# Expert rows scattered to two tables from where they lie, four token tiles summed on TensorE, and constant products placed in ten of TensorE's waits

## The reference, cut to what matters

```python
x = x + mod[:, 2] * (concat([ya, yb, yn]) @ w_out)
h2 = rms_norm_2(x, g2) * (1 + mod[:, 4]) + mod[:, 3]
grp = argmax(h2 @ w_rg + b_rg)                    # one of 4 groups
top_v, top_i = top_k(logit_e[grp], 2)             # 2 of its 8 experts
gate = softmax(top_v) * p_grp
y_e = (silu(g) * u) @ w_down[e],  g, u = split(h2 @ w_up[e])   # 32 experts, hidden 512
f = gate_0 * y_{e0} + gate_1 * y_{e1}             # two experts of each token
out = rms_norm_2(x + mod[:, 5] * f, final_g)
```

## Time and profile before

| What | Value |
|---|---|
| Median of the runs | 2865.32 us (2862.7 to 2867.55) |
| The profiled execution, its own time | 2869.49 us |
| Its span in the profile | 2867.5 us |
| Mean granted TensorE clock | 0.979 |
| TensorE busy | 2743.7 us, 96% |
| VectorE, ACT, POOL busy | 53%, 27%, 3% |
| Moved by DMA | 399.56 MB, 139 GB/s over the span |

### The profile page before, as it was taken

The page is one execution under the profiler, slowest core; times in us unless marked ns, Lnnn a source line. Parts: engine busy times, 40 slices in busy tenths (PEclk is TensorE's granted clock), DMA queues, the critical chain, the costliest instruction groups (busy, mean ns, idle before and its releaser), DMA issues. The chain is left out here.

```text
span 2867.5 us, 44001 instructions
## 1 busy us (share of the span) xinstructions
PE 2743.7 (96%) x18171; PEld 1635.5 (57%) x18171; DVE 1510.6 (53%) x2119; ACT 781.6 (27%) x1449; POOL 83.7 (3%) x138
## 2 busy tenths in 40 slices
PE   8999899999999999999999998999999799999995
PEld 4444554444444444444454445657555699999994
DVE  7886676566666667773652007867683311111114
ACT  2111771111111114511100106757332311211112
POOL 0000000000000000000000000000000011111110
PEclk9999999999999999999999998999999899999997
DMA  3022221111111117764221000004200799999996
GB/s 142 33 74 38 47 90 69 50 44 44 45 44 44 45 50 267 275 240 144 59 61 64 30 0 12 1 1 120 97 12 10 302 395 399 386 403 396 392 397 255
DMA packets 75940, 399.56 MB, mean 139 GB/s; under 512 B 13232, under 2 KB 22960, under 8 KB 59824
## 3 DMA queue, kind: packets, MB, share of 16 engines
q1 hardware_dynamic: 55440, 348.66, 33.1%
q10 hardware_dynamic: 13104, 32.52, 3.2%
q0 software_dynamic: 7280, 16.79, 1.7%
HBM read 362.66 MB, written 29.36 MB: 137 GB/s over the span
## 5 line engine op out<-in xcount | busy, mean ns | idle before, releaser
L3646 PE MATMUL ex_ps<-big,ex_xT 128*32 128x128 f32 x3072 | 348.9, 274 | 0.0
L3644 PE MATMUL ex_ps<-big,ex_xT 128*32 128x384 f32 x3072 | 344.7, 489 | 1.4 <-issue 0.7
L3646 PEld LDWEIGHTS ex_ps<-big,ex_xT 128*32 128x32 f32 x3072 | 333.7, 110 | 0.6
L1756 PE MATMUL ffn_ps<-h,V 128*128 128x512 f32 x504 | 219.7, 592 | 0.0
L2215 PE MATMUL ffn_ps<-big,V 128*128 128x512 f32 x484 | 211.3, 597 | 3.6 <-DVE V L2470 1.4
L296 DVE TENSOR_SCALAR_CACHE_REDUCE h<-ad_s_ps 128x1280 f32<-128x1280 f32 x64 | 92.9, 1489 | 177.2 <-PE ad_s_ps L205 177.2
L3644 PE MATMUL ex_ps<-ex_wd,ex_hT 128*32 128x384 f32 x1536 | 173.4, 492 | 4.3 <-DMA ex_wd<-in_w_edown 1.9
L3646 PE MATMUL ex_ps<-ex_wd,ex_hT 128*32 128x128 f32 x1536 | 175.5, 275 | 0.0
L3646 PEld LDWEIGHTS ex_ps<-ex_wd,ex_hT 128*32 128x32 f32 x1536 | 168.4, 111 | 0.6
L1756 PEld LDWEIGHTS ffn_ps<-h,V 128*128 128x128 f32 x504 | 95.8, 190 | 120.5 <-issue 120.5
L2215 PEld LDWEIGHTS ffn_ps<-big,V 128*128 128x128 f32 x484 | 92.2, 191 | 120.3 <-issue 115.0
(11 more groups left out here) (606 smaller groups left out, 4792.6 us busy)
## 6 DMA issues: line engine op xcount, KB each, us to landing
big<-in_w_eup SPq DMA_DIRECT2D x64, 2048.0 KB, 26.4
ex_wd<-in_w_edown SPq DMA_DIRECT2D x32, 2048.0 KB, 27.4
V<-in_w_down SPq DMA_DIRECT2D x35, 704.0 KB, 5.6
dn_tail<-in_w_mod ACTq DMA_DIRECT2D x48, 512.0 KB, 5.0
fm_up<-in_w_up SPq DMA_DIRECT2D x22, 1028.0 KB, 4.9
dn_tail<-in_w_in SPq DMA_DIRECT2D x17, 512.0 KB, 4.4
big<-y_dram SPq DMA_DIRECT2D x16, 512.0 KB, 7.0
f_w<-in_w_in SPq DMA_DIRECT2D x14, 512.0 KB, 4.3
```

The costliest lines, as they stand in the source:

```text
L1756: mm = nc.tensor.matmul(bank(i, j), wj[:, k, :], bj[:, k, :], start=(k == 0), stop=(k == 3))
L3644: nc.tensor.matmul(o[32 * g:32 * g + 32, 0:W], rows(g), w[:, 0:W], start=first, stop=last)
L3646: mm = nc.tensor.matmul(o[BR:P, g * P:(g + 1) * P], rows(g), w[:, W:BANK], start=first and g == 0, stop=last and g == GR - 1)
```

## The change

Four edits.

1. The table `y_dram` becomes two, `y_wide` with 768 columns and `y_rest` with 256. ACT's moves go. POOL waits for `y_kept` itself and issues four indirect DMAs for a block: one for the 768 columns of 96 rows, three for the 256 columns of 32 rows each, straight from partitions 96 to 127. Their row numbers have to stand at partitions 0 to 31, so route makes them in a second layout (`thirds`: two small turns on TensorE and one VectorE instruction), and POOL copies them beside the others.
2. At the end each tile of 128 tokens is read by two DMAs, and all tiles in the order 0, 4, 1, 5, 2, 6, 3, 7. For tiles 0 to 3 TensorE also sums the second weighted row (`weighted(t, 1, ...)`, with a diagonal of the second gates, `diag1`), and ACT and VectorE take these tiles out of PSUM. VectorE's `mix` remains for tiles 4 to 7.
3. `busy` makes products of two constants of 512 columns whose result nobody reads; it is called at ten places of TensorE's code.
4. `out_rows` moves into a spare part of a large buffer.

```diff
+def busy(nc, cst, bank, count):
+    for _ in range(count):
+        nc.tensor.matmul(bank, cst["ident"], cst["ones_on"], start=True, stop=True)
 attention:
                 scores(0)
+                if packed:
+                    busy(nc, cst, o_banks[0], 3)
                 scores(1)
+                if packed:
+                    busy(nc, cst, o_banks[0], 3)
 ...
                 values(I // 4 - 1)
+                busy(nc, cst, s_ps[:, 0, 0, 0:BANK], 2)
 dilated_attention, at the end:
+                busy(nc, cst, s_ps[:, 0, 0, :], 1)
 near_attention:
                 scores(0)
+                busy(nc, cst, o_ps[:], 1)
                 scores(1)
 front, at the end:
+                wait_kept(pe, J["v", 6])
+                busy(nc, cst, acc[:, J["v", 6] % 2, 0:BANK], 4)
 mid, token_sums:
                     begin(("tok",))
+                    busy(nc, cst, slot(("tok",))[:, 0:BANK], 2)
                     pe.wait_ge(sum_added, KD)
 gla_and_out, at the end:
+                busy(nc, cst, ps[:, 3, :], 2)
 route:
                 nc.tensor.matmul(tot_ps, cst["ones"], total, start=True, stop=True).then_inc(pre_ready, 1)
+                pe.wait_ge(evicted, TT)
+                busy(nc, cst, acc[:, 1, 0:BANK], 7)
 ...
                 nc.tensor.transpose(ids_ps[0:BR], listed[:], cst["ident"][0:NB, 0:NB]).then_inc(ids_ready, 1)
+                for g in range(1, GR):
+                    mm = nc.tensor.transpose(third_ps[0:32, g - 1, 0:NB], listed[:, 32 * g:32 * g + 32], cst["ident"][0:NB, 0:NB])
+                mm.then_inc(ids_ready, 1)
+                busy(nc, cst, acc[:, 1, 0:BANK], 8)
 experts, SP:
-                    for t in (4, 0, 5, 1, 6, 2, 7, 3) if a == 0 else range(TT):
-                        sp.dma_start(f[:, t, :], y_dram[a * T + t * P:a * T + (t + 1) * P, :]).then_inc(got[t], 16)
+                    for t in order:
+                        tile = slice(a * T + t * P, a * T + (t + 1) * P)
+                        sp.dma_start(f[:, t, 0:2 * W], y_wide[tile, :]).then_inc(got[t], 16)
+                        sp.dma_start(f[:, t, 2 * W:D], y_rest[tile, :]).then_inc(got[t], 16)
 experts, POOL, scatter:
+                    nc.gpsimd.tensor_copy(third_at[0:32, u], r["thirds"][0:32, :, bass.ds(i * 2 + u, 1)]).then_inc(row_set, 1)
-                    pool.wait_ge(moved[u], i * (16 * GR) + 16 * GR)
+                    pool.wait_ge(y_kept, i * 2 + (u + 2))
-                    pool.indirect_dma_start(y_dram, bass.IndirectOffsetOnAxis(ap=row_at[0:BR, u:u + 1], axis=0), y[0:BR, u, :], None,
+                    pool.indirect_dma_start(y_wide, bass.IndirectOffsetOnAxis(ap=row_at[0:BR, u:u + 1], axis=0), y[0:BR, u, :], None,
                                             bounds_check=2 * T - 1, oob_is_err=False).then_inc(stored[u], 16)
+                    for g in range(GR):
+                        at = third_at[0:32, u, g - 1, :] if g else row_at[0:32, u:u + 1]
+                        pool.indirect_dma_start(y_rest, bass.IndirectOffsetOnAxis(ap=at, axis=0), y[BR:P, u, g * 2 * P:(g + 1) * 2 * P], None,
+                                                bounds_check=2 * T - 1, oob_is_err=False).then_inc(stored[u], 16)
 experts, TensorE:
+                def weighted(t, a, f, got):
+                    pe.wait_ge(got[t], 32)
                     for half in range(2):
+                        mm = nc.tensor.matmul(sum_ps[t][:, half, :], r["diag1"][t] if a else r["diag"][:, t, :],
+                                              f[:, t, half * BANK:(half + 1) * BANK], start=False, stop=(a == 1))
 experts, ACT:
-                def move_y(i, u):
-                    act.wait_ge(y_kept, i * 2 + (u + 2))
-                    for g in range(GR):
-                        act.dma_start(y[32 * g:32 * g + 32, u, 2 * W:D], y[BR:P, u, g * 2 * P:(g + 1) * 2 * P]).then_inc(moved[u], 16)
 experts, VectorE:
+                for n, t in enumerate(order):
                     if t < PET:
+                        mix(t + PET)
+                    finish(n, t)
```

More of the change, by code:

```diff
@@ L3489, in _, with experts @@
                 V_.tensor_scalar(r["rows"][0:BR, :], ids_ps[0:BR], 2.0 * T, None, ALU.add)
-def experts(nc, tag, cst, din, r, ids, h2_dram, y_dram, wu, u_ready, xb, x_ready, f0, f1, y, hid, a2, shift, h, rows, out):
+                dve.wait_ge(ids_ready, 2)
+                V_.tensor_scalar(r["thirds"][0:32], third_ps[0:32, :, 0:NB], 2.0 * T, None, ALU.add)
+def experts(nc, tag, cst, din, r, ids, h2_dram, tables, wu, u_ready, xb, x_ready, f0, f1, y, hid, a2, shift, h, rows, out):
     H = 512
@@ L3504, in experts @@
         xT = ph.sb("xT", [P, 2, KD, BR])
-        idx, row_at = ph.sb("idx", [P, 2], I32), ph.sb("row_at", [P, 2], I32)
+        idx, row_at, third_at = ph.sb("idx", [P, 2], I32), ph.sb("row_at", [P, 2], I32), ph.sb("third_at", [P, 2, 2, 1], I32)
         W = 4 * BR
+        SCATTERS = 1 + GR
+        y_wide, y_rest = tables
+        order = [t for pair in zip(range(PET), range(PET, TT)) for t in pair]
         hT = ph.sb("hT", [P, GR, P])
@@ L3514, in experts @@
         d_ready = [ph.sem("d_ready0"), ph.sem("d_ready1")]
-        moved, stored = [ph.sem("moved0"), ph.sem("moved1")], [ph.sem("stored0"), ph.sem("stored1")]
+        stored = [ph.sem("stored0"), ph.sem("stored1")]
         got0, got1 = ([ph.sem(f"got{a}_{t}") for t in range(TT)] for a in range(2))
@@ L3568, in _ @@
                     sp.wait_ge(y_free, pairs * 2 + (a + 1))
[L3569 to L3572 removed]
+                    for t in order:
[3 more added lines that the diff above has]
+                for n, t in enumerate(order):
+                    sp.wait_ge(finished, n + 1)
                     sp.dma_start(out[t * P:(t + 1) * P, :], f1[:, t, :]).then_inc(out_stored, 16)
@@ L3734, in _ @@
                 pe.wait_ge(xT_ready, pairs * 2 + 2)
-                token_sum(0)
-                token_sum(1)
-                token_sum(2)
-                pe.wait_ge(y_kept, pairs * 2 + 1)
-                token_sum(3)
+                for t in range(PET):
+                    if t == PET - 1:
+                        pe.wait_ge(y_kept, pairs * 2 + 1)
+                    residual(t)
+                    weighted(t, 0, f0, got0)
+                for t in range(PET):
+                    weighted(t, 1, f1, got1)
             @block.scalar
@@ L3825, in weigh @@
                     V_.tensor_tensor(r["diag"], cst["ident"].unsqueeze(1).broadcast_to([P, PET, P]),
-                                     gate[:, 0, 0:PET].unsqueeze(2).broadcast_to([P, PET, P]), ALU.mult).then_inc(gates_ready, 1)
+                                     gate[:, 0, 0:PET].unsqueeze(2).broadcast_to([P, PET, P]), ALU.mult)
+                    for t in range(PET):
+                        ins = V_.tensor_scalar(r["diag1"][t], cst["ident"], gate[:, 1, t:t + 1], None, ALU.mult)
+                    ins.then_inc(gates_ready, 1)
                 def keep_hidden(i, u):
@@ L3925, in experts_block @@
         h2_dram = nc.dram_tensor("h2_dram", (T, D), F32).ap()
-        y_dram = nc.dram_tensor("y_dram", (2 * T, D), F32).ap()
-        blk, ids, out_rows = keep("blk", [P, NB], I32), keep("ids", [P, NBI], I32), keep("out_rows", [P, NB], I32)
+        y_wide, y_rest = (nc.dram_tensor(x, (2 * T, n), F32).ap() for x, n in (("y_wide", 8 * BR), ("y_rest", D - 8 * BR)))
+        blk, ids = keep("blk", [P, NB], I32), keep("ids", [P, NBI], I32)
         count, first_expert = keep("count", [P, 3], I32), keep("first_expert", [P, 1], I32)
-        small = big[:, 20, 4 * P:4 * P + 9 * TT]
+        small = big[:, 20, 4 * P:8 * P]
         r = {"g4": small[:, 0:4 * TT].rearrange("p (t g) -> p t g", t=TT), "top": small[:, 4 * TT:5 * TT],
-             "gate": small[:, 5 * TT:7 * TT].rearrange("p (a t) -> p a t", a=2), "std": small[:, 7 * TT:8 * TT], "swapped": small[:, 8 * TT:9 * TT], "rows": out_rows[:], "block": blk[:], "count": count[:], "ids": ids[:], "first": first_expert[:],
+             "gate": small[:, 5 * TT:7 * TT].rearrange("p (a t) -> p a t", a=2), "std": small[:, 7 * TT:8 * TT], "swapped": small[:, 8 * TT:9 * TT],
+             "rows": small[:, 9 * TT:9 * TT + NB], "thirds": small[:, 9 * TT + NB:9 * TT + 3 * NB].rearrange("p (g n) -> p g n", g=2),
+             "diag1": [big[:, (18, 21)[t // 2], 8 * BR + t % 2 * P:8 * BR + (t % 2 + 1) * P] for t in range(4)], "block": blk[:], "count": count[:], "ids": ids[:], "first": first_expert[:],
              "gate5": big[:, 18, 0:8 * BR], "final": big[:, 19, :], "diag": big[:, 20, 0:4 * P].rearrange("p (t n) -> p t n", n=P)}
```

68 lines of the change are left out of this document (30 added, 38 removed).

## The result

The changed kernel takes 2928.72 us (median of 4 runs, 2924.65 to 2931.15), the kernel before beside it 2866.44 us (2862.70 to 2871.59): a ratio of 1.0215, 95% interval 1.0194 to 1.0236. I had forecast 2849.5 us. The profiled execution spans 2922.8 us instead of 2867.5, 55.3 us more.

The account below looks back on a forecast made before the run. TensorE bounds the kernel up to 2280 us, TensorE and DMA engines the experts, then a closing chain. 5.9 + 4.7 + 5.3 = 15.9 us won, from a median of 2865.32 to 2849.5 us; range 2841 to 2861.

Parts of the forecast that it names:

- part 1: Expert stage: dropping the moves inside SBUF for four scatters a block relieves the DMA engines and wins 5.9 us.
- 8.2 of 17 us ... Hidden: Expert stage: POOL's four issues, index copies and gather take 8.2 us of a 17 us block, so they stay hidden.
- The third rival: Expert stage: POOL becomes the bound from 3.65 us an issue; at 4.0 us the time is 2897 us; chance 0.05.
- 0.05 for slower: Whole kernel: chance given to a measurement slower than before, against 0.85 for faster and 0.10 for same.
- the range of 2841 to 2861: Whole kernel: forecast range in us, said to leave out the slow case and the far ends.
- DMA relief, 5.9 us: Expert stage: the DMA need falls from 17.5 to 17.3 us a block, so TensorE's whole 5.9 us excess goes.
- the moves' 1.8%: Expert stage: the removed moves' share of DMA time, taken as 9.7 us over 540 us; upper bound 9 us won.
- The end, 4.7 us: After the last y kept: 2.8 us from earlier scatters plus 1.9 us from the tiles; bounds 0 and 7.
- the bare sum: Closing tiles: VectorE takes four pairs at 4.3 us, 17.2 against 21.5, before about 1 us taken back by DMAs.
- my sum: End: the four scatters overlap, the last landing at 2836.0 instead of 2838.84 us, not four times 3.19 us in series.
- Constant products, 5.3 us: TensorE's waits: ad 4.4, near attention, route and mid 1.0 each, less 2.1 at phase ends; bounds -4 and 12.
- Parts 1 and 2: Expert stage scatters, 5.9 us won, and the end after the last y kept, 4.7 us won.

Follow-up runs that it names:

- kernel 8: Changed kernel with each of a block's four scatters let go at its own event, 2 to 6 us apart; 2852.06 us, ratio 0.9942 to the kernel before.
- kernel 12: kernel 8 without any of the constant products; 2854.92 us, ratio 0.9964 to the kernel before.
- kernel 2: The kernel before with the constant products alone added; 2860.04 us, ratio 0.9980 to the kernel before.
- (5): Changed kernel with two scatter issues in a row per block instead of four, same packets and bytes; 2865.45 us (one run).
- (3): Changed kernel with a block's four scatters in two pairs, the second waiting for the next up product; 2877.75 us, ratio 1.0039 to the kernel before.

## Why the prediction was wrong, by its own steps

**The step that failed** is in part 1: "8.2 of 17 us ... Hidden". I priced POOL's four issues as POOL's own time only and put their cost to TensorE at nothing. As POOL's own time the sum was even high: the four take 4.5 us (2331.19 to 2335.65), not 5.8, and POOL is busy 5 us of 19.4. Still the row of four makes the block 2.4 us longer than TensorE's 17.0. From the experts' first turn to the last y kept it is 626.1 us, 63.2 more than before, and 71.6 more than kernel 8 with the same issues apart (554.5, from 2255.48 to 2810.03). The cost stood on an engine whose waits name nothing of POOL's. The third rival, the slow case, had the right instructions and the wrong mechanism: its condition was an issue over 3.65 us, and issues took 0.87 to 0.93 us. So 0.05 for slower was far too low, and its 2897 us rested on a supposed 4.0 us an issue.

What could have warned: nowhere in the rows of before do more than two indirect issues follow each other. The one pair at 1.45 us lies in route, where TensorE waits for another reason, and in the experts two issues are 2.0 us apart. I took from these that issues overlap with everything else. No trace row showed four in a row beside a TensorE fed with short products. So "Hidden" had nothing measured behind it, and the range of 2841 to 2861 left the cost out. How POOL's issues reach TensorE stays open; the runs show that their spacing decides.

**DMA relief, 5.9 us: right.** With the issues apart the period is 17.01 us to the end. In kernel 12 the experts' first turn to the last y kept takes 556.6 us (2255.79 to 2812.36) instead of 562.9, 6.4 us won. One slip of the working: the moves' 1.8% is a share of the 608 us of the earlier trace rows, 10.9 us and not 9.7; it changes the upper bound and not the 5.9.

**The end, 4.7 us: 3.3 in one profile of each kernel, from terms that were each off.** From y kept to the second table's reads it is 11.5 us (2884.57 to SP's read at 2896.10) against 13.0, as the last scatter lands 5.41 us behind its issue, not 3.19: 1.4 us won where I said 2.8. From that read to the first mix it is 5.9 us against 3.3, 2.6 us lost where I said 1.3: the wait ends with the second piece of the second tile, whose read is issued 1.3 us behind the first (2897.41 against 2896.10) and takes 4.47 us where the one before took 3.17. VectorE's part, 2901.97 to 2918.95, is 17.0 us against 21.5, the bare sum: 4.5 us won where I said 3.2, for stores and double DMAs took nothing back. 1.4 - 2.6 + 4.5 = 3.3.

The Trainium skill ("DMA: Bandwidth & Descriptors", Rules for kernel authors) says that many small transfers should be coalesced and that one under 64 KB is mostly overhead. In series, at the 3.19 us of before, that would have been 12.8 us, from 2886.4 to 2899.2; the last landed at 2896.0, so they overlap in part, and the trace stands between the rule and my sum. The loss in the stage is another matter: with 64 bytes a row or 1 KB it is the same 19.39 us a block.

**Constant products, 5.3 us: about 6 us by the ratios (0.2% in kernel 2, and 0.2% between kernels 8 and 12), the mechanism in part unproven.** The scores in ad are as forecast, but kernel 12 has most of that gain without a product. Its experts start at 2255.79 us, earlier than the changed kernel's 2258.46, so the 4.6 us by which these came forward are no measure of the products. One thing was put at nothing and shows: with the 15 products in route the first turn takes 0.85 us instead of 1.51, and kernel 8 needs 2.0 us less than kernel 12 from that turn to the last y kept (554.5 against 556.6).

With the issues spaced the whole is 2852.06 us where the prediction said 2849.5. Parts 1 and 2 alone are some 10 us (kernel 12) where it said 10.6: the gains came about as large as forecast, and one price was missing. That the products' share also came near is in part luck.

## What to carry to other kernels

Several indirect DMAs of POOL in a row can have a price on the other engines, and one that no busy share shows. Beside a TensorE with many short products, hang each on an event of its own, 2 us or more apart, or leave at most two in a row, and look in the profile for idle time named "issue" that follows POOL's issues by 2 us. Where a change adds a kind of row that the trace doesn't show (four issues in a row), time that row by itself before its cost is put at nothing.

## What the runs showed of the hardware

- In the experts TensorE goes on for some 2 us after a row of indirect issues begins. Then, until 2 us after the last starts, it does some 40% of its work: 27 matmul records from 2333 to 2337 us, where 4 us hold 70 at the 17.6 a us of the kernel before (5619 in 320 us).
- In this stage the price follows the number of issues in a row, not rows or bytes: 0.3, 1.3, 2.4 and 6.4 us a block for 2, 3, 4 and 6 (one run each for 2, 3 and 6; with 6 the granted clock is down to 0.88 as well).
- A row of 24 issues (30 us) leaves TensorE, VectorE and ScalarE without work for over 10 us, at a DMA share of 0.08, and q8, an instruction queue, shows no packet until the row has ended. A row of 12 (16 us) did nothing in stretches where TensorE has 5 to 10 records a us.
- Open: in the steady loop of the experts the queues for instructions show no packets between 2400 and 2460 us, neither before nor in the changed kernel, and the changed kernel's TensorE is held up there all the same (busy 55.80 of 60 us). How a loop's instructions reach it, and why issues stand in the way, no run here shows. That two issues in a row cost 0.3 us a block in one kernel (5) and two such pairs 0.6 in another (3) fits the number of pairs, but wasn't taken apart.
